# Row loads of the combining stage issued from inside the experts' stage, into buffers placed over its dead ones

## The reference

```python
def moe_ffn(h, ...):
    ...                                   # sigmoid scores of 64 experts, top 8 of them for each token
    gate = sel / jnp.sum(sel, axis=-1, keepdims=True) * ROUTED_SCALE
    ...
    def expert_block(args):
        xb, e = args
        return (jax.nn.silu(xb @ we_gate[e]) * (xb @ we_up[e])) @ we_down[e]
    ...
    y = yb.reshape(-1, D)[dest] * gate.reshape(-1)[order][:, None]
    routed = jax.ops.segment_sum(y, tok, num_segments=n)
    shared = (jax.nn.silu(t @ ws_gate) * (t @ ws_up)) @ ws_down
    return routed + shared

y = moe_ffn(h, ...)
x = x + gt2 * rmsnorm(y, norm_ffn_post[l])
```

## Time and profile before

| | us |
|---|---|
| median of 3 runs | 1486.5 (1485.4 to 1490.94) |
| the profiled execution, its own time | 1488.43 |
| span of the profiled execution | 1486.7 |
| `combine`, from the release of the meeting to the end of the span | 1434.3 to 1486.7 |

### The profile page before, as it was taken

How to read it: one execution, slowest core, us unless ns; L and a number is a source line. 1 busy time by engine, 2 the same in 40 slices (tenths; PEclk the granted TensorE clock), 3 DMA queues, 4 the chain that set the end, 5 groups by cost and what they waited for, 6 DMA issues and landing times. The chain is left out here.

```text
span 1486.7 us, 18817 instructions
## 1 busy us (share of the span) xinstructions
PE 1351.9 (91%) x5795; PEld 926.4 (62%) x5795; DVE 1046.8 (70%) x1651; ACT 613.1 (41%) x931; POOL 347.0 (23%) x350
## 2 busy tenths in 40 slices
PE   5799999974889799996899999999999999999947
PEld 3577677632779444443676776767767677676713
DVE  4539999968753253363688888888888888888617
ACT  3322212134224211212465655656656566565502
POOL 0243424233000000001222232322323223232200
PEclk9799999887789899998899999999999999999969
DMA  8434443210000461133599999999999999998358
GB/s 303 153 135 149 177 163 114 85 71 0 2 1 1 193 240 77 64 142 152 222 342 357 344 357 353 359 344 349 376 393 358 347 344 354 355 355 293 133 221 351
DMA packets 85266, 339.26 MB, mean 228 GB/s; under 512 B 16918, under 2 KB 20176, under 8 KB 58084
## 3 DMA queue, kind: packets, MB, share of 16 engines
q1 hardware_dynamic: 65400, 304.97, 54.5%
q0 software_dynamic: 19584, 33.60, 6.2%
q10 hardware_dynamic: 236, 0.09, 0.0%
HBM read 332.31 MB, written 44.04 MB: 253 GB/s over the span
## 5 line engine op out<-in xcount | busy, mean ns | idle before, releaser
L2158 DVE TENSOR_TENSOR gate_up_low<-gate_up,gate_up_high 128x1024 fp32r<-128x1024 f32 x204 | 244.7, 1220 | 42.2 <-ACT gate_up_high L2049 42.2
L2130 PE MATMUL py<-down_ring,hT 128*128 128x512 f32 x544 | 250.0, 602 | 0.9 <-ACT hT L2068 0.9
L2091 PE MATMUL p_gate_up<-gate_up_high,x_hi 128*128 128x512 f32 x544 | 242.7, 446 | 5.3 <-DVE x_lo L2167 5.3
L2091 PE MATMUL p_gate_up<-gate_up_low,x_hi 128*128 128x512 f32 x544 | 217.1, 399 | 0.0
L2091 PE MATMUL p_gate_up<-gate_up_high,x_lo 128*128 128x512 f32 x544 | 215.9, 397 | 0.0
L2049 ACT ACTIVATE gate_up_high<-gate_up 128x1024 fp32r<-128x1024 f32 x204 | 203.7, 1051 | 0.6 <-PEq L1308 0.6
L2130 PEld LDWEIGHTS py<-down_ring,hT 128*128 128x128 f32 x544 | 98.0, 190 | 98.8 <-issue 98.7
L2020 POOL TENSOR_TENSOR carrier<-offsets 1x1 f32<-1x1 f32 x136 | 29.2, 215 | 522.1 <-DVE tokens L2176 475.2
L269 POOL TENSOR_TENSOR ring_lo<-ring,w_hi 128x2048 fp32r<-128x2048 f32 x19 | 91.5, 4814 | 179.3 <-ACT w_hi L310 179.3
L2091 PEld LDWEIGHTS p_gate_up<-gate_up_high,x_hi 128*128 128x128 f32 x544 | 104.1, 191 | 45.1 <-issue 21.4
L429 PE MATMUL pz<-h_hi,w_hi 128*128 128x512 f32 x304 | 123.4, 406 | 7.7 <-DVE h_lo L497 7.7
(11 more groups left out here) (359 smaller groups left out, 2038.2 us busy)
## 6 DMA issues: line engine op xcount, KB each, us to landing
down_ring<-in_we_down SPq DMA_DIRECT2D x68, 1024.0 KB, 9.6
gate_up<-in_we_gate SPq DMA_DIRECT2D x51, 1024.0 KB, 7.0
gate_up<-in_we_up SPq DMA_DIRECT2D x51, 1024.0 KB, 9.8
ring<-in_w_ada SPq DMA_DIRECT2D x12, 2048.0 KB, 7.9
ring<-in_w_in SPq DMA_DIRECT2D x9, 2048.0 KB, 10.1
x_again<-in_we_gate SPq DMA_DIRECT2D x17, 1024.0 KB, 7.0
x_again<-in_we_up SPq DMA_DIRECT2D x17, 1024.0 KB, 9.8
rows<-expert_rows SPq DMA_DIRECT2D x6, 2048.0 KB, 18.3
```

The source lines that it names most:

```text
L2091: mm = pe.matmul(pgu[u % 2][:, :], x[:, u % 2, k, :], weights, start=(k == 0 and n == 0), stop=(k == KD - 1 and n == 2))
L2130: mm = pe.matmul(py[half][:, :], hT[:, u % 2, k, :], weights[:, k, half * N:half * N + N], start=(k == 0), stop=(k == 1))
L2158: V.tensor_tensor(moe.low[u % RING][:, :, piece(i), :], moe.gate_up[u % RING][:, :, piece(i), :], exact(w_hi[:, u % 2, :, piece(i), :]), A ...
```

## The change

Line numbers of the changed kernel are 13 to 16 higher from L1871 on. `load_rows` does what the ten issues at the start of `combine` did, in the same order and shapes. It is called by SP at the end of its `experts` stream: the wait for x1 is gone, and SP waits instead until GpSimd has started all scatters (`s_scatter`) and has signalled, after its loop, that they have landed (`s_landed`). The destination `row_tiles` is laid out ahead of the experts' buffers at the address that `rows6` had; a placeholder keeps that memory in `combine`. The semaphores of the row loads and of x1 are allocated in `layer`. DVE waits for x1 in `finish`.

```diff
+    expert_rows = moe.rows.rearrange("(t p j) d -> t p j d", p=P, j=TOPK)
+
+    def load_rows(engine):
+        H, LAST = TOPK // 2, NT - 1
+        for t in range(LAST):
+            for j, landed in ((0, moe.s_pe_in), (H, moe.s_dve_in)):
+                engine.dma_start(moe.row_tiles[:, t, j:j + H, :], expert_rows[t][:, j:j + H, :]).then_inc(landed[t], 16)
+        for half in range(2):
+            cs = slice(half * N, half * N + N)
+            for j, landed in ((0, moe.s_pe_in), (H, moe.s_dve_in)):
+                engine.dma_start(moe.row_tiles[:, LAST, j:j + H, cs],
+                                 expert_rows[LAST][:, j:j + H, cs]).then_inc(landed[LAST + half], 16)
...
@@ experts, sync
             sp.wait_ge(s_y, count)
-            sp.dma_start(moe.x1[:, :, :], keep.x1_dram.rearrange("(t p) d -> p t d", p=P)).then_inc(s_x1, 16)
-            sp.wait_ge(s_x1, 16)
+            sp.dma_start(moe.x1[:, :, :], keep.x1_dram.rearrange("(t p) d -> p t d", p=P)).then_inc(moe.s_x1, 16)
+            sp.wait_ge(s_scatter, count)
+            sp.wait_ge(s_landed, 1)
+            moe.load_rows(sp)
@@ experts, gpsimd
             steps(pool, [(4, gather), (0, scatter)], lambda b, u: scattered(pool, b, u))
+            pool.sem_inc(s_landed, 1)
@@ combine
-        rows = m.sb("rows6", [P, NT, TOPK, D])
-        x1 = moe.x1
+        m.sb("rows_kept6", [P, NT, TOPK, D])
+        rows, x1 = moe.row_tiles, moe.x1
...
@@ combine, sync
-            for t in range(LAST):
-                sp.dma_start(rows[:, t, 0:H, :], expert_rows[t][:, 0:H, :]).then_inc(s_pe_in[t], 16)
-                sp.dma_start(rows[:, t, H:TOPK, :], expert_rows[t][:, H:TOPK, :]).then_inc(s_dve_in[t], 16)
-            for half in range(2):
-                sp.dma_start(rows[:, LAST, 0:H, cols(half)], expert_rows[LAST][:, 0:H, cols(half)]).then_inc(s_pe_in[LAST + half], 16)
-                sp.dma_start(rows[:, LAST, H:TOPK, cols(half)],
-                             expert_rows[LAST][:, H:TOPK, cols(half)]).then_inc(s_dve_in[LAST + half], 16)
@@ combine, vector, finish
                 dve.wait_ge(s_r, t + 1)
+                dve.wait_ge(s_x1, 16)
@@ layer
+        with ExitStack() as last_use:
+            moe.row_tiles = Memory(nc, last_use).sb("rows6", [P, NT, TOPK, D])
+        moe.s_pe_in = [m.sem(f"p6_tensor_rows{t}_in") for t in range(NT + 1)]
+        moe.s_dve_in = [m.sem(f"p6_vector_rows{t}_in") for t in range(NT + 1)]
+        moe.s_x1 = m.sem("p6_x1_in")
```

More of the change, by code:

```diff
@@ L1872, in load_down @@
         engine.dma_start(moe.down[:, slot, :, :], of(last, expert)).then_inc(moe.s_down[slot], 16)
-    moe.load_gate_up, moe.load_down = load_gate_up, load_down
+    expert_rows = moe.rows.rearrange("(t p j) d -> t p j d", p=P, j=TOPK)
[9 more added lines that the diff above has]
+                                 expert_rows[LAST][:, j:j + H, cs]).then_inc(landed[LAST + half], 16)
+    moe.load_gate_up, moe.load_down, moe.load_rows = load_gate_up, load_down, load_rows
 def experts(nc, w, keep, moe):
@@ L1914, in experts @@
         s_y, s_yA, s_yV = m.sem("p5_down"), m.sem("p5_y_by_scalar"), m.sem("p5_y_by_vector")
-        s_x1 = m.sem("p5_x1_in")
+        s_landed = m.sem("p5_all_rows_landed")
         s_out = [m.sem(f"p5_scattered{i}") for i in range(2)]
@@ L2214, in combine @@
         bank = [m.bank(f"e{i}") for i in range(2 * NT)]
-        s_pe_in = [m.sem(f"p6_tensor_rows{t}_in") for t in range(NT + 1)]
-        s_dve_in = [m.sem(f"p6_vector_rows{t}_in") for t in range(NT + 1)]
+        s_pe_in, s_dve_in, s_x1 = moe.s_pe_in, moe.s_dve_in, moe.s_x1
         s_sum = m.sem("p6_tensor_sum")
@@ L2224, in combine @@
         block = stack.enter_context(nc.Block())
-        expert_rows = moe.rows.rearrange("(t p j) d -> t p j d", p=P, j=TOPK)
         LAST = NT - 1
```

## The result

| | before | after |
|---|---|---|
| median us | 1488.24 (4 runs, 1485.4 to 1490.94) | 1506.82 (4 runs, 1505.21 to 1507.18) |
| ratio | | 1.012, 95% interval 1.010 to 1.014 |
| profiled execution, span | 1486.7 | 1505.1 |

What follows compares the result with a forecast made beforehand. Row loads of combine were taken as the critical path (30.8 us wait). PE starts 29.4 us later (31.5 hold, 0.5 meeting, less 2.6), 9.3 given back: 20.1 us over the median 1486.5 gives 1506.6 us, range 1501 to 1513.

Steps and rivals of the forecast that it cites:

- Start of the loads: SP's first row load at the end of experts is issued at 1431.8 instead of 1434.38, 2.6 us earlier.
- rival C: Signal reaches SP only behind GpSimd's 2.44 us drain, loads not earlier: 1509 us; chance counted within the forecast's 0.86.
- The hold: SP, issuing the ten row loads ahead of the meeting, is held for the same 31.5 us, until 1463.3.
- The meeting: From SP being free to PE's start in combine, with branch and drain: 0.5 us, so PE starts at 1463.8.
- The slow clock: PE starts combine at a lower clock after long idling: 2.2 us charged once, up to 1.5 more as bound.
- PE's 4.29 us for each half: PE's work in combine: six half tiles to the end of tile 2, 25.7 us, ending at 1491.7.
- DVE 0.1 us behind: In combine DVE needs 8.3 us a tile against PE's 8.6, so it follows PE by 0.1 us.
- 14.9 us of tile 3: From DVE's second addition of tile 2 to the span's end, tile 3 and last store: 14.9 us, unchanged.
- The sum: Span of the whole kernel: 1491.7 + 0.1 + 0.1 + 14.9 = 1506.8 us, 20.1 above 1486.7.
- A: SP's ten issues are not held ahead of combine, taking 0.48 us each: 1484 us, within 0.5%; chance 0.08.
- break-even: Hold of SP ahead of the meeting at which the change neither gains nor loses: 11.4 us.
- B: SP's hold is shorter without readers, 15 to 25 us: 1490 to 1500 us; chance 0.03 slower, 0.01 no change.

Runs made afterwards that it cites:

- eight_ahead: Changed kernel with only the first eight of ten row loads ahead of the meeting, the last two at the start of combine: 1486.47 us, ratio 0.9999.
- coarse_last: Changed kernel with tile 3 in two loads of 2 MB instead of four of 1 MB, all loads ahead of the meeting: 1488.59 us, ratio 1.0007.
- nine_ahead: Changed kernel with nine row loads ahead of the meeting and the tenth at the start of combine: 1505.73 us in a single run.
- early_ten: Changed kernel with GpSimd's signal ahead of its empty turns, all ten row loads ahead of the meeting: 1503.32 us in a single run.
- seven_ahead: Changed kernel with only the first seven row loads ahead of the meeting, the last three at the start of combine: 1486.52 us, ratio 1.0005.
- seven_again: The same kernel as seven_ahead, run again with more rounds: 1484.16 us, ratio 0.9988.
- early_seven: Changed kernel with seven row loads ahead of the meeting and GpSimd's signal ahead of its empty turns: 1479.79 us, ratio 0.9946.
- before_fine: Kernel before the change with all four tiles in 1 MB loads by column halves (2 KB packets), nothing moved: 1494.8 us in a single run.
- before_coarse: Kernel before the change with tile 3 in two loads of 2 MB (16 KB packets), nothing moved: 1491.26 us in a single run.

## Why the prediction was right

It forecast 1506.6 us, 20.1 us above the median then known; measured were 1506.82, which is 18.6 above that of the four runs. The mechanism was right, but that the two totals agree to 0.2 us is in part luck: the loss was forecast 1.5 us too large, and the median that it is added to came out 1.7 us higher. The steps:

- *Start of the loads, 2.6 us earlier.* From the issue of x1 to the first load it is 1430.99 - 1417.98 = 13.0 us, and was 15.6. Right. GpSimd's signal passed ahead of its drain, and rival C fell.
- *The hold, 31.5 us.* 1462.07 - 1430.99 = 31.1. It was taken over on the ground that the same DMAs go into the same queue. That held: the longest hold is the same to 0.01 us, the eighth and ninth issue together take 25.3 us as before, and only the tenth is shorter, 2.3 us and not 2.8.
- *The meeting, 0.5 us.* 1462.51 - 1462.07 = 0.44.
- *The slow clock, 2.2 us.* The first half tile took 1468.49 - 1462.51 = 5.98, less 4.29: 1.7. The granted clock was 0.50 from 1460 to 1465 and 0.92 in the next 5 us:

```profile
1460.00:1465.00 5.00, 2.49 (x3) 1.17 (x4) 2.46 (x2) 0.00 (x0) 0.00 (x0) 0.50 0.95 361
1465.00:1470.00 5.00, 5.00 (x12) 2.24 (x11) 1.74 (x2) 0.52 (x1) 0.00 (x0) 0.92 1.05 393
```

- *PE's 4.29 us for each half, DVE 0.1 us behind, 14.9 us of tile 3.* PE ends tile 2 at about 1490.1 (forecast 1491.7), DVE's second addition of tile 2 starts at 1490.22, and the span ends 1505.1 - 1490.2 = 14.9 later:

```profile
1490.22 0.69 DVE L2303 TENSOR_TENSOR y<-rows,e 128x512 f32<-128x512 f32 x1 [0.55 <-PE e L2260]
```

- *The sum.* 1506.8 forecast for the span, 1505.1 measured. The 1.7 us are the 0.8 by which the last down product came earlier in this execution, 0.4 of the hold, 0.5 of the clock, and under 0.1 of the meeting.

Of the rivals, A (no hold without readers) is refuted by the changed kernel itself: no engine read a tile before 1462.5, and the holds were the same. Its break-even, a hold of 11.4 us, was right: eight_ahead has 11.0 and loses nothing. B (a shorter hold) fell with it. The section of the Trainium skill named there (DMA: Bandwidth & Descriptors, Anatomy of one DMA) says that many descriptors can be emitted before the cost shows, but its heading is for DMAs that GpSimd issues; taking it over to those of SP was a step of the prediction. The first seven issues, 0.33 to 0.54 us each, and all eight in coarse_last agree with it; the eighth to tenth, 7.6, 17.6 and 2.3 us, do not.

Two readings of the prediction were inexact without weight for the sum. 1475.76 is when PE's last rows had landed; DVE's last load, issued at 1463.08, landed at about 1478.4, still far ahead of 1490. And PE is not nine tenths busy from the start of the experts' stage on: its first gather is at about 696 us, and the slice from 707 to 744 shows 8.

What I named to look for came out, with one exception. The first store was at 1476.30, forecast near 1478. The exception is that the wait of PE was not put down to SP: the profile names PE's own sequencer at L1895, the line of the block's end. Who is late there is read from the drains of that line, of which SP's comes last.

## What to carry to other kernels

A DMA issue is not free when the queue is full of packets (0.33 to 0.54 us here when it is not, up to 17.64 when it is), and it then holds everything behind it in the issuing engine's stream. Before DMAs are moved ahead of a point where all engines meet, read the durations of their issues in the trace: those that return at once can go ahead, those that are held are better left behind, where nobody waits for the issuer. A hold ahead of the meeting costs what it takes beyond the slack, which was some 11 us here. And ask what the signal that lets them start stands behind: passing seven empty loop turns of GpSimd took 4.3 us off the tail, passing the meeting itself 2.5.

## What the runs showed of the hardware that was not expected

- A queue fills by packets and not by bytes: 16 MB in 16 KB packets went in within 3.89 us, while with 2 KB packets the fifth MB was held. The trace counts 9315 packets in before_fine and 2307 in before_coarse between 1430 and 1490, for the same row loads (with seven stores in the first and eight in the second):

```profile
DMA packets 9315, 18.38 MB, mean 306 GB/s; under 512 B 352, under 2 KB 352, under 8 KB 9312
```

```profile
DMA packets 2307, 18.91 MB, mean 315 GB/s; under 512 B 256, under 2 KB 256, under 8 KB 1280
```

- The rate differs too: 386 to 388 GB/s with the 2 KB packets of before_fine (columns of the earlier trace rows), 423 to 441 with the 16 KB packets of before_coarse. One stretch of each:

```profile
1450.00:1460.00 10.00, 9.90 (x21) 4.11 (x20) 5.88 (x6) 1.85 (x6) 0.00 (x0) 0.89 1.05 387
```

```profile
1454.00:1464.00 10.00, 9.34 (x23) 3.95 (x22) 7.96 (x10) 1.84 (x6) 0.55 (x1) 1.00 1.00 424
```

- The longest held issue is nearly the same with or without engines that read: 17.64 us before, 17.64 after, 17.65 in nine_ahead and 17.64 in early_ten, and within 0.01 us of that in seven_ahead, seven_again and early_seven. Only eight_ahead differs, with 17.29; why stays open.
- GpSimd's drain at the end of the block took 2.442 us before, after and in early_seven alike, though in early_seven it ran beside the row loads in full and before it ran with no DMA under way.
